# Top-k threshold search on VectorE: a table of next candidates in place of a base and three new candidates in each pass

## The reference

```python
def expert_choice_ffn(h, p):
    b, n, d = h.shape
    cap = CAPACITY_FACTOR * n // N_EXPERTS          # 256
    logits = jnp.einsum('bnd,de->bne', h, p['router']).astype(jnp.float32)
    probs = jax.nn.softmax(logits, axis=-1)
    gate, idx = lax.top_k(probs.transpose(0, 2, 1), cap)
    xs = jax.vmap(lambda hb, ib: hb[ib])(h, idx)
    ...
```

## Time and profile before

| | |
|---|---|
| median of 3 runs | 2242.05 us (2239.07 to 2243.31) |
| profiled execution: its own time | 2250.38 us |
| profiled execution: span from first to last instruction | 2248.7 us |
| TensorE busy | 95% of the span |
| VectorE busy | 70% |
| ScalarE busy | 43% |
| GpSimd busy | 20% |
| mean granted TensorE clock | 0.97 of full |
| the 15 passes | 1156.4 to 1189.4 us of the span |
| end of the stage's work on VectorE | 1197.8 us |
| first matmul of the experts | about 1213 us |

### The profile page before, as it was taken

The page is one execution under the profiler, slowest core; times in us unless marked ns, Lnnn a source line. Parts: engine busy times, 40 slices in busy tenths (PEclk is TensorE's granted clock), DMA queues, the critical chain, the costliest instruction groups (busy, mean ns, idle before and its releaser), DMA issues. The chain is left out here.

```text
span 2248.7 us, 37421 instructions
## 1 busy us (share of the span) xinstructions
PE 2126.0 (95%) x14325; PEld 1397.7 (62%) x14325; DVE 1577.7 (70%) x2224; ACT 977.8 (43%) x1343; POOL 440.5 (20%) x448
## 2 busy tenths in 40 slices
PE   6899999999999999899966999999999999999995
PEld 3344444444778787645524777777777777777773
DVE  3659999785679797865566666666666666766666
ACT  3521002364656556545542444443444444443344
POOL 1420001011546565300022011101111011101111
PEclk8999999999999999999987999999999999999998
DMA  9251002455010211375544888777887888777786
GB/s 351 79 100 33 20 19 89 127 157 147 25 53 15 87 53 30 120 267 173 178 173 156 266 244 261 242 243 246 260 244 250 253 249 266 242 234 254 249 269 264
DMA packets 280294, 392.90 MB, mean 175 GB/s; under 512 B 101507, under 2 KB 142979, under 8 KB 279693
## 3 DMA queue, kind: packets, MB, share of 16 engines
q1 hardware_dynamic: 261770, 333.10, 45.5%
q0 software_dynamic: 16528, 56.47, 9.0%
q10 hardware_dynamic: 1908, 2.18, 0.3%
HBM read 313.44 MB, written 62.54 MB: 167 GB/s over the span
## 5 line engine op out<-in xcount | busy, mean ns | idle before, releaser
L91 PE MATMUL pgu<-xhi,mwlo 128*128 128x256 bf16 x2048 | 558.2, 273 | 0.0
L90 PE MATMUL pgu<-xlo,mwhi 128*128 128x256 bf16 x2048 | 558.2, 273 | 0.0
L89 PE MATMUL pgu<-xhi,mwhi 128*128 128x256 bf16 x2048 | 558.2, 273 | 0.0
L2547 DVE TENSOR_TENSOR mwlo<-mwst,mwhi 128x2048 bf16<-128x2048 f32 x187 | 426.8, 2282 | 0.0
L2447 ACT ACTIVATE mwhi<-mwst 128x2048 bf16<-128x2048 f32 x186 | 350.8, 1901 | 9.6 <-DMA mwst<-in_w_gate 9.6
L2455 ACT ACTIVATE thb<-pgu 128x256 f32<-128x256 f32 x128 | 49.0, 383 | 544.3 <-PE pgu L91 544.2
L731 DVE SCALAR_TENSOR_TENSOR co<-u,taps,co 128x1984 f32<-128x1984 f32 (+22 forms) x120 | 234.1, 1951 | 3.7
L2558 DVE SCALAR_TENSOR_TENSOR thb<-thb,pgu 128x256 f32<-128x256 f32 x128 | 53.7, 419 | 244.8 <-ACT thb L2455 244.8
L89 PEld LDWEIGHTS pgu<-xhi,mwhi 128*128 128x128 bf16 x2048 | 200.3, 98 | 24.6
L90 PEld LDWEIGHTS pgu<-xlo,mwhi 128*128 128x128 bf16 x2048 | 200.3, 98 | 24.3
L91 PEld LDWEIGHTS pgu<-xhi,mwlo 128*128 128x128 bf16 x2048 | 200.4, 98 | 23.4
(11 more groups left out here) (389 smaller groups left out, 4064.8 us busy)
## 6 DMA issues: line engine op xcount, KB each, us to landing
mwst<-in_w_gate SPq DMA_DIRECT2D x32, 2048.0 KB, 9.1
mwst<-in_w_up SPq DMA_DIRECT2D x32, 2048.0 KB, 8.1
mwst<-in_w_down SPq DMA_DIRECT2D x32, 2048.0 KB, 11.2
wst<-in_w_in SPq DMA_DIRECT2D x28, 512.0 KB, 6.5
big<-in_ada_w SPq DMA_DIRECT2D x5, 2048.0 KB, 18.1
s_rows<-row SPq DMA_DIRECT2D x16, 520.0 KB, 5.6
u<-in_ada_w SPq DMA_DIRECT2D x8, 1024.0 KB, 6.3
xt<-in_x SPq DMA_DIRECT2D x16, 512.0 KB, 4.3
```

The lines of the kernel that those rows point to most:

```text
L89: nc.tensor.matmul(out, lh, rh, start=(first and k == 0), stop=False)
L90: nc.tensor.matmul(out, lh, rl, start=False, stop=False)
L91: ins = nc.tensor.matmul(out, ll, rh, start=False, stop=(last and k == n - 1))
L2547: nc.vector.tensor_tensor(wlo[:, b, ks], wst[:, b % NS, ks], whi[:, b, ks], ALU.subtract)\
```

## The change

A pass no longer makes a base first and three candidates from it. `cand` holds four candidates, the base itself as number 0. While the counts are under way, a `table` of 4 x 4 entries is made: entry (j, i) is candidate i with the bits j of the next pass set. When the totals are there, one masked step over all 16 entries (line 2216 in the new kernel) zeroes the entries whose candidate i has a total under 256, and one maximum over i (line 2219) gives the four candidates of the next pass at once. Candidate 0 has no count of its own: its column in `cnt4` is set once to 256 per partition, and the count matmul has 4 columns. The last pass has one row of the table only, and its maximum is the threshold. Ahead of the first pass stand two memsets and three instructions that make the first candidates. Line numbers above 2144 move by up to 10.

```diff
--- before.py
+++ after.py
@@ -2142,9 +2142,10 @@
         cg = near.sb("cg", [P, W])
         ce = near.sb("ce", [P, W])
         slot = near.sb("slot", [P, W])
-        cand = near.sb("cand", [P, 2, 3])
-        cnt3 = near.sb("cnt3", [P, 2, 3], BF16)
-        acc = near.sb("accp", [P, 2, 4])
+        cand = near.sb("cand", [P, 2, 4])
+        table = near.sb("table", [P, 4, 4])
+        kept = near.sb("kept", [P, 4, 4])
+        cnt4 = near.sb("cnt4", [P, 2, 4], BF16)
         cnt = near.sb("cnt", [P, 2], BF16)
         base = near.sb("base", [P, 4])
         sT = near.sb("sT", [P, NE, NCK, 2])
@@ -2153,8 +2154,8 @@
         pc2 = m.ps("pc2", [P, SEG])
         ptr = m.ps("ptr", [P, 4, P])
 
-        col_ok, c_ok, cnt_ok, tot, a_ok, t_ok = (m.sem("tcol_ok"), m.sem("tc_ok"), m.sem("tcnt"), m.sem("ttot"),
-                                                 m.sem("ta_ok"), m.sem("tt_ok"))
+        col_ok, c_ok, cnt_ok, tot, tab_ok, k_ok = (m.sem("tcol_ok"), m.sem("tc_ok"), m.sem("tcnt"), m.sem("ttot"),
+                                                   m.sem("ttab"), m.sem("tk_ok"))
         grow = near.sb("grow", [1, 2, SEG])
         g_ps, g_sb, g_out = SEL.g_ps, m.sem("g_sb"), m.sem("g_out")
         fin, ofs, slo, trp, ve = m.sem("tfin"), m.sem("tofs"), m.sem("tslo"), m.sem("ttrp"), m.sem("tve")
@@ -2191,26 +2192,33 @@
 
             @block.vector
             def _(dve):
-                nc.vector.memset(acc[:, 0, 3:4], 0.0).then_inc(t_ok, 1)
+                nc.vector.memset(cnt4[:, :, 0:1], float(W)).then_inc(tab_ok, 1)
+                nc.vector.memset(cand[:, 0, 0:1], 0.0).then_inc(tab_ok, 1)
+                dve.wait_ge(tab_ok, 2)
+                for j in range(1, 4):
+                    nc.vector.tensor_scalar(cand[:, 0, j:j + 1].bitcast(U32), cand[:, 0, 0:1].bitcast(U32),
+                                            j << (2 * (STEPS - 1)), None, ALU.bitwise_or).then_inc(tab_ok, 1)
+                dve.wait_ge(tab_ok, 5)
                 for b in range(STEPS):
-                    p = b % 2
-                    dve.wait_ge(t_ok, b + 1)
+                    p, rows = b % 2, 4 if b < STEPS - 1 else 1
+                    if b:
+                        dve.wait_ge(c_ok, b)
                     for j in range(3):
-                        nc.vector.tensor_scalar(cand[:, p, j:j + 1].bitcast(U32), acc[:, p, 3:4].bitcast(U32),
-                                                (j + 1) << (2 * (STEPS - 1 - b)), None, ALU.bitwise_or).then_inc(c_ok, 1)
-                    for j in range(3):
-                        dve.wait_ge(c_ok, 3 * b + j + 1)
                         if b >= 1:
                             dve.wait_ge(cnt_ok, 3 * b + j - 2)
-                        nc.vector.tensor_scalar(tmp[:, j], pr[:], cand[:, p, j:j + 1], None, ALU.is_ge, ALU.add,
-                                                accum_out=cnt3[:, p, j:j + 1]).then_inc(cnt_ok, 1)
+                        nc.vector.tensor_scalar(tmp[:, j], pr[:], cand[:, p, j + 1:j + 2], None, ALU.is_ge, ALU.add,
+                                                accum_out=cnt4[:, p, j + 1:j + 2]).then_inc(cnt_ok, 1)
+                    for j in range(rows):
+                        nc.vector.tensor_scalar(table[:, j].bitcast(U32), cand[:, p].bitcast(U32),
+                                                j << max(0, 2 * (STEPS - 2 - b)), None, ALU.bitwise_or).then_inc(tab_ok, 1)
+                    dve.wait_ge(tab_ok, 5 + 4 * b + rows)
                     dve.wait_ge(tot, b + 1)
-                    nc.vector.scalar_tensor_tensor(acc[:, p, 0:3], pc[:, 4 * p:4 * p + 3], float(CAP), cand[:, p],
-                                                   ALU.is_ge, ALU.mult).then_inc(a_ok, 1)
-                    dve.wait_ge(a_ok, b + 1)
-                    nc.vector.tensor_reduce(acc[:, 1 - p, 3:4], acc[:, p], AX.X, ALU.max).then_inc(t_ok, 1)
-                thr = acc[:, STEPS % 2, 3:4]
-                dve.wait_ge(t_ok, STEPS + 1)
+                    nc.vector.scalar_tensor_tensor(kept[:, 0:rows], pc[:, 4 * p:4 * p + 4].unsqueeze(1).broadcast_to([P, rows, 4]),
+                                                   float(CAP), table[:, 0:rows], ALU.is_ge, ALU.mult).then_inc(k_ok, 1)
+                    dve.wait_ge(k_ok, b + 1)
+                    nc.vector.tensor_reduce(cand[:, 1 - p, 0:rows], kept[:, 0:rows], AX.X, ALU.max).then_inc(c_ok, 1)
+                thr = cand[:, STEPS % 2, 0:1]
+                dve.wait_ge(c_ok, STEPS)
                 nc.vector.tensor_scalar(gt[:], pr[:], thr, None, ALU.is_gt, ALU.add, accum_out=cnt[:, 0:1])\
                     .then_inc(fin, 1)
                 nc.vector.tensor_scalar(eq[:], pr[:], thr, None, ALU.is_equal, ALU.add, accum_out=cnt[:, 1:2])\
@@ -2252,8 +2260,10 @@
             def _(pe):
                 for b in range(STEPS):
                     p = b % 2
+                    if b == 0:
+                        pe.wait_ge(tab_ok, 5)
                     pe.wait_ge(cnt_ok, 3 * b + 3)
-                    nc.tensor.matmul(pc[:, 4 * p:4 * p + 3], same[:], cnt3[:, p], start=True, stop=True).then_inc(tot, 1)
+                    nc.tensor.matmul(pc[:, 4 * p:4 * p + 4], same[:], cnt4[:, p], start=True, stop=True).then_inc(tot, 1)
                     late = 2 * KD - SEL.EARLY
                     SEL.second_gate(nc, pe, K, range(SEL.EARLY + b * late // STEPS, SEL.EARLY + (b + 1) * late // STEPS))
                 pe.wait_ge(fin, 2)
```

## The result

The changed kernel is slower: 2255.86 us median of 4 runs (2254.17 to 2258.52) against 2242.68 us of 4 runs of the kernel before (2239.07 to 2245.66). The ratio is 1.0052 with a 95% interval of 1.0038 to 1.0066, that is 8.5 to 14.8 us. The forecast was 2240.8 us.

A forecast was written before the change was run, and what follows sets the result against it. VectorE's own chain, with one TensorE round trip, was taken to bound a 2.15 us pass. 13 x -0.105 = -1.37 us plus 0.18 for setup gave -1.2, from 2242.05 to 2240.8 us; range 2237.4 to 2244.2.

The forecast's parts named there:

- Added: four table instructions, behind the third count: Between last read and masked step: four table instructions stick out of the 0.37 us round trip by 0.05 us a pass.
- the slower one: Rival, chance 0.08: between third sum and masked step the tables run one after another, +2.9 us, 2245.0 us.
- The setup: Ahead of the first pass: first count waits for all three candidates, plus a second memset, together +0.18 us.
- The gain of a pass: Each VectorE-bound pass: candidates removed, wider masked step and tables added, about -0.105 us, in 13 of 14 gaps.
- The maximum to the count: Within a pass: the count follows the maximum directly, 0.22 us instead of 0.39, a gain of 0.17 us.
- A table instruction 147 to 161 ns: Behind the third count: length of one table instruction, bounded by the candidate and another TENSOR_SCALAR over 4 elements.
- four of them in 0.35 to 0.40 us: Behind the third count: the four table instructions overlap, the fourth ending 0.35 to 0.40 us after the last read's start.
- The masked step: After the tables in each pass: starts about 0.42 us behind the third read's start, not 0.37, released by the table.
- Hidden tables with the full clock at the end: Lower bound of all cases: tables wholly covered by the round trip and TensorE's final instructions at full clock, -3.0 us.
- The clock: Rival, chance 0.27: TensorE's granted clock decides at pass 4 to 5 and the end, adding -1.7 to +0.85 us.
- the pass from 4 to 5: Gap between passes 4 and 5: set by TensorE's product and bias row, keeps its 2.83 us and gains nothing.
- TensorE's tail: From last count matmul to the offsets: stays 3.58 us and sets the stage's end; full clock would return up to 1.7.

The follow-up runs named there:

- the second profile of the kernel before: The kernel before, unchanged, profiled a second time: 2244.86 us, with the stage from first memset to the experts' first matmul at 55.13 us.
- the second pair: The changed kernel, unchanged, run a second time against the kernel before: 2255.78 us median of 5 against 2243.95, ratio 1.0055.

## Why the prediction was wrong

**The step that failed** is "Added: four table instructions, behind the third count". It let them cost what sticks out from the round trip to TensorE, 0.05 us a pass, with an upper bound of 0.17. That holds in 12 of 14 gaps (a gain of 0.095 us each, forecast 0.105). In the two beside GpSimd's conversions they cost 6.39 and 5.99 us over the usual 2.05, 12.4 us together. The bound was made from the lengths of like instructions in the trace, and the cover was looked for on VectorE and TensorE alone; what runs on GpSimd meanwhile was named (the weights "had their conversions done in the passes") and priced at nothing. None of the rivals has this mechanism, and the slower one (tables end to end, +2.9 us) had the place right and neither the cause nor the size.

What the trace before had shown was there to see: 16.15 us of GpSimd reading SBUF in the middle of the passes. The VectorE instructions of the passes before are all of forms that are not held beside it: one element, the form with an accumulator, one PSUM operand, a reduction. But an earlier stage of the same trace has the hold. There VectorE copies 16 elements a partition from SBUF to SBUF (tile `sm`), and this is one of the copies, with GpSimd's instruction beside it and the view of the whole line (ns min/median/max):

```profile
663.74 2.26 POOL L1170 TENSOR_TENSOR of<-of,rsb 128x512 f32<-128x512 f32 x1
...
664.97 1.06 DVE L1365 COPY sm<-B 128x16 f32<-128x16 f32 x1
...
L1365 DVE COPY sm<-B x40: 170/176/1065, 557.2 to 921.7; 128x16 f32<-128x16 f32 x32, 128x8 f32<-128x8 f32 x8
```

The usual copy takes 0.18 us. Five of the 40 start inside a GpSimd instruction; they take 0.95 to 1.07 us, and each ends 0.03 us behind the end of that instruction. A price for a small instruction within SBUF beside GpSimd could have been read there.

**The sum, with the hold in it.** The passes grow by 41.10 - 30.03 = 11.07 us against the second profile of the kernel before: +12.38 held, and -1.3 of gain (28.71 against 30.03 where nothing is held). The setup, from the memset to the first count matmul, takes 1.88 us (1149.94 to 1151.82) for 1.63 (1152.61 to 1154.24), +0.25. With 0.2 us at the tail (23.7 for 23.5) the stage is 66.66 - 55.13 = 11.5 us longer, and the whole is 11.7 us longer by the ratio, 12.3 in the second pair. Nothing is left over that the runs can tell.

**What was right.** The gain of a pass: forecast 0.105 us, measured 2.145 - 2.05 = 0.095. The maximum to the count: forecast 0.22, measured 0.20. A table instruction 147 to 161 ns: 164 in the median; four of them in 0.35 to 0.40 us: 0.38. They overlap, and the rival that had them end to end fell in every kernel. (Against this overlap stood a sentence of the Trainium skill, VectorE: DVE Perf Modes, The DRAIN you can't avoid. The same section adds that an instruction that does not have to wait for the earlier ones to finish starts earlier, and this trace agrees, with a new table instruction each 0.07 us.) The setup: the first count was forecast 0.18 us later behind the memset, measured 0.44 for 0.28 us, +0.16; the first count matmul comes another 0.09 us later, which the forecast did not have and no run took apart. The masked step: forecast 0.42 us behind the read, measured 0.44. But its reason was only half right: with the table out of the way the same 0.29 us behind the count matmul stayed until the two waits changed places, so the tables' end and the order of the waits each led to the same time.

**Two sums of the prediction** don't come out. Hidden tables with the full clock at the end are -1.8 - 1.7 = -3.5 us, not -3.0. And the lower end of the range is counted from 2242.05 (less 2.9 and 1.7), the upper is not: 2242.05 + 0.8 + 2.6 is 2245.4, not 2244.2. The measured 2255.86 is beyond either.

**The clock** was given 0.27, and the two places named are the ones where it showed: -0.7 us in the pass from 4 to 5 (2.14 for 2.84) and -1.7 in TensorE's tail between two profiles of one kernel. Two consequences were missed. At full clock the pass from 4 to 5 is VectorE's like the others, so 14 gaps gain. And then TensorE's tail is no longer last: in the changed kernel's profile the offsets matmuls start at 1194.92 and 1194.96 us and VectorE's scans end at 1196.16, so what happens in VectorE's last pass does count, and of the 1.7 us only 0.8 came through.

## What to carry to other kernels

A VectorE instruction put beside GpSimd's work is priced by its form first and its length second: one within SBUF over several elements (4 and 16 here), or with two inputs in SBUF, can wait for the whole of a GpSimd instruction, whatever its own 0.16 us. Before adding one to a chain, look in the trace for what GpSimd does in that stretch, and for the longest instruction of that form, not the mean, wherever GpSimd works. Then keep one operand in PSUM (nothing is held here), or the element count at one as the candidates have it; element counts between 1 and 4 were not tried. Shorter GpSimd instructions help less: halves took the loss in the passes from 12.4 to 9.0 us. And of two waits on one instruction the one that ends last is written first, if it is known.

## What the runs showed of the hardware

- The hold is by whole instructions, and follows their length (4.04 us with conversions of 4.05, 2.10 with 2.12). Of four table instructions in a row the first was held to the end of the running conversion and the third for the whole of the next, in all eight passes that met a conversion (two in each profile of the changed kernel, four with the half conversions). The second and the fourth started 0.01 to 0.03 us before the next conversion did, or behind the last one, and took 0.16 us.
- GpSimd's side was longer too: beside scans and masked steps with two SBUF inputs its conversions took up to 4.43 us for 4.06. That it was held in its turn is the likely reading and was not tested by itself.
- Not held beside the conversions: 128x1 from SBUF to SBUF (143 to 154 ns), four elements from PSUM to SBUF (146 to 157 ns), four elements from one PSUM and one SBUF input (155 to 173 ns).
- Four small independent VectorE instructions of 164 ns take 0.38 us together, a new one each 0.07 us.
- Two waits on one VectorE instruction: 0.29 us from the matmul's start with the earlier event waited for first, 0.22 us with the later one first (0.20 to 0.23 over the passes).
- One short table of one instruction ahead of a wait: 0.65 us for 0.29 in the last pass, unexplained.
